# The MLP of an encoder layer: first product by Strassen's seven block products on two halves of 768 tokens, in place of a plain product on three blocks of 512

## The reference, cut to what matters

```
D_MODEL = 1024; D_FF = 4 * D_MODEL
...
    x = x + merged @ w_out

    h = rms_norm(x, norm_mlp)
    x = x + jnp.square(jax.nn.relu(h @ w_ff1)) @ w_ff2
```

## Time and profile before

| | |
|---|---|
| time, median of three runs (lowest to highest) | 2534.86 us (2534.62 to 2536.88) |
| span of the profiled execution, first to last instruction | 2532.5 us |
| what lies around the span, against the lowest and the median run | 2.1 to 2.4 us |
| PE busy / weight loads busy | 99% / 81% of the span |
| DVE, ACT, POOL busy | 64%, 42%, 49% |
| DMA | 282 MB, 111 GB/s mean |
| granted clock of PE | full (0.999) |
| the tail | from about 1096 us to the end |

### The profile page before, as it was taken

How to read it: one execution, slowest core, us unless ns; L and a number is a source line. 1 busy time by engine, 2 the same in 40 slices (tenths; PEclk the granted TensorE clock), 3 DMA queues, 4 the chain that set the end, 5 groups by cost and what they waited for, 6 DMA issues and landing times.

```text
span 2532.5 us, 37844 instructions
## 1 busy us (share of the span) xinstructions
PE 2512.6 (99%) x11168; PEld 2059.1 (81%) x11168; DVE 1611.6 (64%) x1809; ACT 1064.8 (42%) x1553; POOL 1230.5 (49%) x850
## 2 busy tenths in 40 slices
PE   8999999999999999999999999999999999999999
PEld 6888888888777777778888888888888888888887
DVE  7986688888888888876654353667354346663351
ACT  7554112121777777854433232344233233432231
POOL 0005664644667676654444444444444444444444
PEclk9999999999999999999999999999999999999999
DMA  5444233334542222143323345423233454232333
GB/s 183 173 168 162 93 92 87 88 87 113 134 116 73 52 58 48 34 156 124 98 93 99 97 129 178 163 98 97 95 99 101 152 178 135 98 98 93 100 95 121
DMA packets 151237, 282.07 MB, mean 111 GB/s; under 512 B 47728, under 2 KB 60528, under 8 KB 151024
## 3 DMA queue, kind: packets, MB, share of 16 engines
q1 hardware_dynamic: 151152, 281.00, 35.5%
HBM read 222.10 MB, written 48.76 MB: 107 GB/s over the span
## 4 chain that ended last, share of the span: by engine, by line
PE 97%; DMA 1%; ACT 1%; issue 1%; SPq 0%; DVE 0%; POOL 0%; DVEq 0%; POOLq 0%; ACTq 0%
PE banks L63 22%; PE banks L65 22%; PE banks L64 22%; PE p_acc L63 3%; PE p_acc L65 3%; PE p_acc L64 3%; PE banks L1899 3%; PE banks L1900 3%; PE banks L1868 3%; PE banks L1853 3%; PE banks L1848 3%; PE banks L1847 3%; PE banks L1457 1%; PE banks L1465 1%; PE banks L1438 0%
## 5 line engine op out<-in xcount | busy, mean ns | idle before, releaser
L2121 POOL TENSOR_TENSOR t_wlo<-t_wraw,t_whi 128x1024 fp32r<-128x1024 f32 x265 | 670.1, 2529 | 774.6 <-ACT t_whi L2139 774.6
L63 PE MATMUL banks<-block,t_whi 128*128 128x512 f32 x1920 | 748.6, 390 | 0.8 <-issue 0.8
L65 PE MATMUL banks<-block,t_wlo 128*128 128x512 f32 x1920 | 747.0, 389 | 0.0
L64 PE MATMUL banks<-block,t_whi 128*128 128x512 f32 x1920 | 746.9, 389 | 0.0
L2139 ACT ACTIVATE t_whi<-t_wraw 128x1024 fp32r<-128x1024 f32 x265 | 280.4, 1058 | 615.4 <-PE banks L65 557.6
L63 PEld LDWEIGHTS banks<-block,t_whi 128*128 128x128 f32 x1920 | 360.4, 188 | 77.5 <-issue 2.8
L64 PEld LDWEIGHTS banks<-block,t_whi 128*128 128x128 f32 x1920 | 360.4, 188 | 75.3 <-issue 0.7
L65 PEld LDWEIGHTS banks<-block,t_wlo 128*128 128x128 f32 x1920 | 360.4, 188 | 74.9
L1698 POOL TENSOR_TENSOR a_plo<-a_p,a_phi 128x512 fp32r<-128x512 f32 x239 | 308.5, 1304 | 142.6 <-DVE a_phi L1816 131.6
L2327 DVE TENSOR_TENSOR t_x<-banks,t_x 128x512 f32 (+1 forms) x96 | 66.4, 692 | 371.7 <-PE banks L65 371.7
L2321 DVE TENSOR_TENSOR block<-t_tc,block 128x512 f32 x96 | 234.2, 2439 | 28.9 <-ACT block L2212 28.4
(11 more groups left out here) (261 smaller groups left out, 3914.7 us busy)
## 6 DMA issues: line engine op xcount, KB each, us to landing
t_wraw<-w_tail_t SPq DMA_DIRECT2D x266, 512.0 KB, 3.5
block<-roped_scratch SPq DMA_DIRECT2D x144, 128.0 KB, 2.7
w_raw<-w_in_t SPq DMA_DIRECT2D x31, 512.0 KB, 3.8
proj_scratch<-s_gate SPq DMA_DIRECT2D x48, 256.0 KB, 2.1
t_graw<-proj_scratch SPq DMA_DIRECT2D x24, 512.0 KB, 3.7
p_sw<-p_qn SPq DMA_DIRECT2D x60, 128.0 KB, 2.0
roped_scratch<-p_r_hi SPq DMA_DIRECT2D x30, 256.0 KB, 2.2
roped_scratch<-p_r_lo SPq DMA_DIRECT2D x30, 256.0 KB, 2.3
```

Of the source, the lines that this page charges most:

```text
L63: pe.matmul(out, whi, xhi, start=start, stop=False)
L64: pe.matmul(out, whi, xlo, start=False, stop=False)
L65: return pe.matmul(out, wlo, xhi, start=False, stop=stop)
L2121: pool.tensor_tensor(w_lo[s][:], w_raw[s][:], f32(w_hi[s][:]), ALU.subtract).then_inc(wlo_ready, 1)
```

## The change

The merges and output projections of all three blocks now come first; their results go to memory (`x1_scratch`, `normed_scratch`, the second with gain and norm factor already applied, for blocks 0 and 1). Then the MLP runs over two halves of 768 tokens.

Within a half, the first product takes two output tiles (a "pair", 16 per half) at a time. Weights, inputs and outputs are cut in two both ways: token quarters are `QN` = 384 columns, the 1024 inputs are two groups of `KH` = 4 tiles. Seven block products (`d` = 0 to 6, each 4 k x 3 = 12 matmuls of 128x384) take the place of eight. Their left operands are blocks or sums of blocks of the weights (`weight_sum`, four DVE subtractions or additions of 128x512 per pair), their right operands sums of quarters of the activations, prepared once per half (`quarter_sums`, `quarter_low`). The results are put together from PSUM: three snapshots by ACT (`snap`), three additions, four relu (ACT), four multiplications for the square, four high parts (ACT), four low parts (DVE). The second product stays plain: per pair of pairs a "group" of eight items, each 2 (halves of 384 columns) x 4 k x 3 = 24 matmuls of 128x384. An item's weights are now 128x512 (4 tiles of k), in a ring of four. All 224 low parts of first-product items are made by DVE (`LOW_ON_DVE` names all seven), the 128 of second-product items by POOL. In all 2688 + 3072 = 5760 matmuls of 128x384.

Loops (`Fori`) of the tail are written out. The order of items in one half: pair 0; then (pair, pair, group) six times; then three pairs and two groups.

```diff
+class Feed:
+    def __init__(self):
+        self.items, self.start, self.group_at = [], {}, {}
+        for h in range(2):
+            self.pair(h, 0)
+            for g in range(FF_PAIRS // 2 - 2):
+                self.pair(h, 2 * g + 1)
+                self.pair(h, 2 * g + 2)
+                self.group(h, g)
+            for p in range(FF_PAIRS - 3, FF_PAIRS):
+                self.pair(h, p)
+            for g in range(FF_PAIRS // 2 - 2, FF_PAIRS // 2):
+                self.group(h, g)
...
+    def pair(self, h, p):
+        self.start[h * FF_PAIRS + p] = len(self.items)
+        self.items += [Item("f1", h, p, d) for d in range(7)]
...
+            def weight_sum(pg, i):
+                u = feed.unit[feed.start[pg]]
+                m1, m2 = ring_raw[u % 4], ring_raw[(u + 1) % 4]
+                n = 4 * pg
+                if i == 0:
+                    unit_in(dve, u)
+                    unit_in(dve, u + 1)
+                    if pg:
+                        f_low_done(dve, feed.start[pg - 1] + S1)
+                    dve.tensor_tensor(sums[0][:], m2[:, 0:KH], m2[:, KH:KD], ALU.add).then_inc(s_ready.sem, 1)
...
+            for t in range(END + 3):
+                if 0 < t <= END and feed.items[t - 1].kind == "f2":
+                    evict(t - 1, 1)
+                for pg, d in feed.pairs_near(t, 4, 8):
...
+                    if d < 7:
+                        f1_done.wait(dve, 7 * pg + d)
+                    if d == 4:
+                        snapped.wait(dve, 3 * pg + 3)
+                        dve.wait_ge(alo_ready, 4 * pg)
+                        dve.tensor_tensor(z12, w, snap[2][:], ALU.add).then_inc(c_done.sem, 1)
+                    elif d == 5:
+                        dve.tensor_tensor(z22, x, snap[1][:], ALU.add).then_inc(c_done.sem, 1)
+                    elif d == 6:
+                        dve.tensor_tensor(y, y, snap[0][:], ALU.add).then_inc(c_done.sem, 1)
+                        squared(0, 1, 1)
...
+                for pg, d in feed.pairs_near(t, -6, -3):
+                    if pg:
+                        weight_sum(pg, d + 6)
...
+                if t + 3 < END and feed.on_dve(t + 3):
+                    f_low(t + 3)
+                if t < END and feed.items[t].kind == "f2":
+                    evict(t, 0)
...
+            for t in range(END):
+                it, s = feed.items[t], t % 4
+                pe.wait_ge(f_hi_ready, t + 1)
+                if feed.on_dve(t):
+                    lo_dve.wait(pe, len(ON_DVE) + feed.dve_before[t + 1])
+                else:
+                    lo_pool.wait(pe, feed.pool_before[t + 1])
+                if it.kind == "f1":
...
+                    elif d in (2, 3, 4):
+                        snapped.wait(pe, 3 * pg + d - 1)
+                    elif d == 5 and pg:
+                        pe.wait_ge(alo_ready, 4 * pg)
+                    elif d == 6:
+                        c_done.wait(pe, 7 * pg + 2)
...
+                    for k in range(KH):
+                        out, last = ps[:, bank, 0:QN], k == KH - 1
+                        x_hi, x_lo = place[d, k, 0], place[d, k, 1]
+                        pe.matmul(out, ring_hi[s][:, k], x_hi, start=fresh and k == 0, stop=False,
+                                  skip_group_check=True)
+                        pe.matmul(out, ring_hi[s][:, k], x_lo, start=False, stop=False, skip_group_check=True)
+                        mm = pe.matmul(out, ring_lo[s][:, k], x_hi, start=False, stop=last, skip_group_check=True)
+                    mm.then_inc(f1_done.sem, 1)
```

And at the end of SP's work for the last block, where `x1_ready` counts additions out of PSUM to the residual:

```diff
+                    if m % 2:
+                        sp.wait_ge(x1_ready, b * KD + m + 3)
+                        sp.dma_start(two_tiles(x1_d, b, m // 2), x1[:, m - 1:m + 1]).then_inc(x1_out.sem, 16)
+            load_unit(2)
+            load_unit(3)
```

More of the change, by code:

```diff
@@ L1959, in tail @@
[L1959 to L1969, removed]
@@ new lines, in tail @@
+        ta = [msb(f"t_ta{s}", [P, BLK]) for s in range(2)]
+        tb = [msb(f"t_tb{s}", [P, BLK]) for s in range(2)]
+        tc = [msb(f"t_tc{s}", [P, BLK]) for s in range(2)]
+        merge_ctx.close()
+        fsb = lambda name, shape, dt=F32: ctx.enter_context(nc.sbuf_tensor(name, shape, dt))
+        x1f = fsb("f_x1", [P, KD, HALF])
+        sums = [fsb(f"f_s{i}", [P, KH, P]) for i in range(4)]
+        snap = [fsb(f"f_snap{i}", [P, QN]) for i in range(4)]
+        with nc.sbuf_tensor("f_t4", [P, KH, QN], F32) as t4:
+            pass
@@ new lines, in tail @@
+        third = fsb("f_a2", [P, 8, QN], F32R)
+        rs2 = st.stage[1][:, 0:BLK]
+        relu = {(0, 1): st.stage[1][:, BLK:BLK + QN], (1, 1): st.stage[1][:, BLK + QN:BLK + 2 * QN],
+                (0, 0): st.stage[1][:, BLK:BLK + QN], (1, 0): snap[3][:]}
+        A_BANK, G_BANK, O_BANK, MEAN = 0, 4, 2, 2
+        X_BANK, W_BANK, Y_BANK, F2_BANK, A12_BANK, A22_BANK = 0, 4, 5, 2, 6, 7
+        cells = lambda t, n0, n1: [t[:, i * QN:(i + 1) * QN] for i in range(n0, n1)]
+        b0, b1, b2 = fore.block
@@ new lines, in tail @@
+        early = cells(b0, 11, 21) + cells(b1, 11, 21) + cells(b2, 0, 21)
+        for v in fore.v:
+            early += cells(v.rearrange("p k h d -> p (k h d)"), 0, 5)
+        late = cells(b0, 0, 11) + cells(b1, 0, 11)
+        place = {(c, kt, i): early[12 * kt + 2 * c + i] for c in range(6) for kt in range(KH) for i in range(2)}
+        place.update({(T4, kt, i): late[2 * kt + i] for kt in range(KH) for i in range(2)})
+        left = late[8:] + early[48:]
+        a_cells = [left[0:8], left[8:16], [third[:, i] for i in range(8)]]
@@ L2063, in one_block @@
-            def one_block(b, more_blocks):
-                blk = bass.ds(b * BLK, BLK)
-                def merge_pair(i, more, third_in=False):
-                    for s in range(2):
[L2068 to L2092, removed]
-                            sp.wait_ge(f2_added, b * (4 * KD) + 2 * i + (3 * KD + s + 3))
-                            alone(sp, sp_turn)
-                            sp.dma_start(y_t[b][:, 2 * i + s], x1[:, 2 * i + s]).then_inc(y_out, 16)
-                    if c is not None:
-                        mix_chunk(b + 1, c)
-                if more_blocks:
```

885 lines of the change are left out of this document (613 added, 272 removed).

## The result

The change takes 2519.82 us (median of 4 runs, 2517.22 to 2522.16) against 2534.74 us (4 runs) for the kernel before: ratio 0.9941, 95% interval 0.9927 to 0.9955. It is faster by 15 us, half of what I forecast (31). Its profiled execution took 2517.22 us with a span of 2515.4 us, 17.1 us less than the span before; it was the fastest of its four. One run in experiment 6 took 8801 us and is left out there.

A forecast was written before the change was run, and what follows sets the result against it. PE's matmuls were taken to bound the tail: the span 2532.5 - 55 + 3 + 3 + 4 + 7.5 + 7 = 2502.0, with the time around it 2504 us; range 2475 to 2555.

The forecast's parts named there:

- The pace: MLP matmuls: 171.7 ns each at 384 columns, so 1044.2 us become 989.0, a term of -55 us.
- the weight load as a bound: Rival in the MLP: loads of 188 ns set the matmul pace, 2594 us in all; chance 7%.
- The merges and output projections ... 0, cover the 43.5 us of matmuls: Merges and output tiles: same 1728 matmuls, next block's input preparation fits under 43.5 us of them; term 0.
- Block 2's output tiles: Entry part (a): DVE, partly waiting for POOL, about 1.1 us late for each of four; +4 us.
- The entry: Entry part (b): pair 1's weights load behind the last x1 store, delaying DVE's sum and z22 for item 6; +7.5 us.
- the signs that I had named for being wrong: PE waiting before most items, squares L2723 much over 0.56 us, lower clock behind the entry's wait, or late weight loads.
- The middle pairs: Middle one of three adjacent MLP pairs: DVE late, 4 x 0.7 = +3 us, and +3 more in pair 1 of half 0.
- the rival of DVE making PE wait in every pair: DVE's order delays all 32 pairs, 2574 us at 2.5 us each; 10% slower, 7% no change, 8% smaller loss.
- Between the halves: Groups 6 and 7 of half 0: DVE late preparing the other half, 1.5 us for each of four; +7 us.
- the band of 2515 to 2530 us: Case of a smaller loss from DVE's order making PE wait in every pair; chance 8%.

The follow-up runs named there:

- experiment 6: The change with pair 1's loads earlier, x1 stores later, second-half low parts dealt 1, 3, 3, and each step's second sum moved to its second item: 2501.14 us, ratio 0.9872.
- experiment 1: The kernel before with its MLP sections cut to other shapes, output not the layer's: 227 ns per matmul at 512 columns, 173 at 384, 120 at 256, 112 at 128.
- experiment 3: The change with SyncE's stores of x1 and their wait moved behind the next weight load, in all three blocks: 2510.07 us, ratio 0.9907.
- experiment 2: The change with the loads of pair 1's two weight tiles moved before the last store of x1 on SyncE: 2513.36 us, ratio 0.9923.
- experiment 7: The change with three of each pair's seven low weight parts made by POOL and four by DVE: 2518.08 us, ratio 0.9947.

## Why the forecast was right and wrong

**The pace: mechanism right, size off by 8.4 us.** The term "5760 x 0.1717 = 989.0 us" took the middle between a share in proportion and one per matmul; it is one per matmul (173.2 ns, experiment 1), so the term is -46.6 us. This is the first of the two steps that failed. The choice of a middle was the error: the float32 passes in the trace of the kernel before, 162 ns at 192 columns and 109 at 128 (L1449) for 160 and 107 ns of streaming, already showed an addition that does not grow with the columns, only of another size. Worked out with the measured pace, the change is two: cutting 512 columns to 384 with eight products would be 6144 x 0.1732 = 1064 us, 20 us more than before, and leaving out the eighth takes 66.5 us away.

**Against the weight load as a bound: right.** The loads are busy 100% of the MLP and yet do not bound; the rule of Perfetto Trace Analysis in the Trainium skill (section Identifying the Most-Contended Engine), in its measure by the busy share of the loads, would have read this as no headroom, but loads 192 ns long started every 120 ns at 256 columns in experiment 1.

**"The merges and output projections ... 0, cover the 43.5 us of matmuls": the second step that failed**, by 9 us in the change's profile and by some 5 to 9 over four profiles. I counted the work of ACT and DVE, which does fit, and neither SP's program order nor how long a load takes to land. In blocks 0 and 1 SP issues most weight loads 2.1 to 3.0 us after their buffer is free, mainly because it waits for an input chunk's low part first, and they take 4.4 to 8.0 us to land where the median was 3.5 before. What each of the two costs PE stays open; the wait for the addition to x1 was not shown to cost anything there (experiment 3).

**Block 2's output tiles: about right in size (4 for 6), for the wrong cause.** I had DVE late behind POOL, and in the trace DVE idles 5 to 6 us per two tiles there, and ACT 7, for weights. Each second tile SP waits for the addition to x1 before it issues the next weight load, and experiment 3 takes 4 to 6 us away by moving that wait.

**The entry: right in size (7.5 for 7.6) and in cause**, shown by experiment 2; wrong in the way. The wait fell on item 4 by ACT's snapshot, not on item 6 by z22, and a third of its price is the halved clock behind it. Both were among the signs that I had named for being wrong: weight loads that come late, and a clock that falls behind the entry's wait.

**The middle pairs: +6 forecast, 0 measured.** I added 0.03 us to each DVE operation's busy time. In the trace, operations that do not depend on each other overlap. DVE at the entry, from the change's timeline:

```profile
1494.94 0.69 DVE L2616 TENSOR_TENSOR f_s<-a_quotient 128x512 f32<-128x512 f32 x1
1495.54 0.69 DVE L2620 TENSOR_TENSOR t_wlo<-a_quotient,t_whi 128x512 fp32r<-128x512 f32 x1
1496.14 0.69 DVE L2620 TENSOR_TENSOR t_wlo<-f_s,t_whi 128x512 fp32r<-128x512 f32 x1
```

They start 0.60 us apart at 0.69 us each (and 0.47 at 0.56 for 384 columns), so a pair is 11 x 0.60 + 11 x 0.47 = 11.8 us against PE's 14.5, not 14.5 against 14.4. The operations that read and write PSUM (L2723) took no more than the others, so the rival of DVE making PE wait in every pair is out, and experiment 7 agrees. (Its price was set a little wrong: at 1.0 us a pair, -55 + 32 + 15 still leaves 8 us of gain; it is gone at 1.25.)

**Between the halves: right** (7 for 6) in size and in place: the first item of each step, and DVE held up behind POOL.

In sum the direction and most places were right; the gain was forecast twice too high because a pace was averaged where it should have been decided, and because the weight loads of the output tiles were not followed from issue to landing. That the waits came near in sum (24.5 us forecast, 30.3 measured) is in part luck: 6 us that did not come at the middle pairs stood for some of those that came elsewhere. The time also lies in the band of 2515 to 2530 us that I had given 8%, but for DVE making PE wait in every pair, which is not what happened.

## What to carry to other kernels

Before a change of tile shape, split the pace of a matmul in streaming and what comes once per matmul, and count matmuls, not only columns: here a quarter more matmuls at 13 ns each took back 20 of 66 us. When a stage moves, follow the queue that issues the DMAs row by row: at the entry and in block 2 a wait for a result in front of the next weight load made engines idle that each had time enough. Look also at how long the loads take to land when other transfers move into their stage. On PE a wait can cost more than itself: at or behind the three of 2.0, 3.2 and 4.4 us in the change's output tiles and entry, the granted clock fell to half. And take a second profile before a few us are put down to an edit: here the same code differed by 3.5 us in the same tiles.

## What the runs showed of the hardware

- A float32r matmul with a new weight load has, at full clock, some 13 to 15 ns that do not depend on the columns, from 512 down to 256; at 128 columns it took 112 ns. A float32 pass has 2 ns in the same place. What the 13 ns are was not found; fewer weight columns did not shorten them. At half clock they are not there: from 1509.8 to 1514.9 us of the change, matmuls of 384 columns start exactly 320 ns apart, which is 384 columns at 1.2 GHz.
- Weight loads of 188 to 192 ns follow each other every 173 ns in the change, where they show as 100% busy, and every 120 ns in experiment 1: they did not bound.
- DVE operations that do not depend on each other start 0.60 us apart at 128x512 (0.69 us each) and 0.47 apart at 128x384 (0.56 each).
- Loads of 512 KB that landed in 3.5 us (median) before took 5.5 (median of eight, 1180 to 1230 us) and 6.6 (median of four, 1330 to 1358 us) where input chunks and stores moved beside them.
- In the probe's section of 128 columns the granted clock fell to a mean of 0.56, although PE was busy 37.87 of 39.10 us by the trace; most matmuls there start 213 ns apart, for 107 ns of streaming at half clock:

```profile
2168.20:2197.80 29.60, 24.25 (x193) 23.27 (x193) 8.96 (x11) 9.59 (x10) 19.54 (x8) 1.00 0.45 142
2234.40:2273.50 39.10, 37.87 (x193) 37.77 (x193) 8.90 (x11) 9.17 (x10) 19.26 (x8) 0.56 0.34 108
```

The first line is the section of 256 columns, with more idle time and a full clock.
